# A second, transposed copy of x for 31 of the 48 token tiles of a hybrid encoder layer on eight cores

## The reference

```
def _rmsnorm(x, g):
    y = x * rsqrt(mean(x * x, axis=-1) + 1e-6) * g

hn = _rmsnorm(x, norm_g)
proj = einsum('bsd,de->bse', hn, w_in)
q, k, v, z_a, hc, gb, gc, z_b, g = split(proj)
...
u = gc * hc
conv = conv_w[0] * up[:, :-2] + conv_w[1] * up[:, 1:-1] + conv_w[2] * up[:, 2:]
c = (silu(z_b) * (gb * conv)) @ w_conv_out
```

## Time and profile before

| | |
|---|---|
| median of 3 runs | 1511.72 us (1510.96 to 1669.54) |
| the profiled execution | 1512.84 us, slowest core's span 1511.3 us |
| spans of the eight cores | 1508.7 to 1511.3 us |
| PE busy | 98% of the span |
| DVE, ACT, POOL busy | 62%, 46%, 10% |
| convolution steps | from about 27 us to about 270 us of the span |

### The profile page before, as it was taken

The page is one execution under the profiler, slowest core; times in us unless marked ns, Lnnn a source line. Parts: engine busy times, 40 slices in busy tenths (PEclk is TensorE's granted clock), DMA queues, the critical chain, the costliest instruction groups (busy, mean ns, idle before and its releaser), DMA issues.

```text
span 1511.3 us, 28483 instructions; the slowest of 8 cores (1508.7 to 1511.3 us)
## 1 busy us (share of the span) xinstructions
PE 1476.7 (98%) x11360; PEld 847.4 (56%) x11360; DVE 930.4 (62%) x1493; ACT 697.5 (46%) x1169; POOL 144.4 (10%) x286
## 2 busy tenths in 40 slices
PE   4999999999999999999999999999999999999997
PEld 2454445577666666675866665766444444444443
DVE  4677777335775848667569575686854444445445
ACT  4445454344575656645356557465322322232222
POOL 5212113000010000100000000001100000000001
PEclk9999999999999999999999999999999999999999
DMA  9964554413151431512425115154943233243233
GB/s 253 153 125 103 117 106 78 72 39 83 29 104 18 96 56 26 95 16 40 87 63 104 29 23 107 26 101 67 190 105 101 84 107 91 82 111 101 67 112 125
DMA packets 67764, 132.07 MB, mean 87 GB/s; under 512 B 8752, under 2 KB 34480, under 8 KB 67376
## 3 DMA queue, kind: packets, MB, share of 16 engines
q1 hardware_dynamic: 49296, 96.70, 23.8%
q0 software_dynamic: 18336, 33.56, 16.3%
HBM read 130.17 MB, written 33.62 MB: 108 GB/s over the span
## 4 chain that ended last, share of the span: by engine, by line
PE 90%; DMA 4%; DVE 3%; issue 1%; ACT 1%; POOL 1%; SPq 0%; DVEq 0%; POOLq 0%; ACTq 0%
PE ps L407 53%; PE ps L702 10%; PE ps L1092 7%; PE ps L1122 6%; PE ps L858 6%; PE ps L722 4%; PE ps L811 3%; DMA X<-w_in 2%; PE ps L452 1%; DMA gc_s<-X 1%; DMA X<-xw 1%; DVE X L908 1%; DVE X L833 0%; POOL stat L421 0%; SPq L163 0%
## 5 line engine op out<-in xcount | busy, mean ns | idle before, releaser
L407 PE MATMUL ps<-hnT,wbf 128*128 128x512 bf16 (+1 forms) x3008 | 666.2, 374 | 1.8 <-ACT X L397 0.8
L407 PEld LDWEIGHTS ps<-hnT,wbf 128*128 128x128 bf16 x3008 | 282.4, 98 | 312.1 <-issue 2.9
L397 ACT ACTIVATE X<-ps 128x512 bf16<-128x512 f32 (+2 forms) x320 | 219.4, 694 | 198.0 <-PE ps L407 157.6
L823 ACT ACTIVATE X<-ps 128x512 bf16<-128x512 f32 x384 | 204.3, 615 | 116.8 <-PE ps L811 116.8
L407 PE MATMUL ps<-hnT,X 128*128 128x512 bf16 (+1 forms) x1152 | 245.6, 367 | 0.1
L873 DVE TENSOR_TENSOR X<-ps,X 128x512 f32<-128x512 f32 x128 | 110.9, 867 | 157.8 <-PE ps L858 118.4
L407 PEld LDWEIGHTS ps<-hnT,X 128*128 128x128 bf16 x1152 | 107.9, 98 | 125.6 <-DMA X<-w_in 0.5
L1097 DVE SCALAR_TENSOR_TENSOR hnT<-hnT,ps 128x512 f32<-128x512 f32 x128 | 87.0, 685 | 146.5 <-PE ps L1092 145.0
L833 DVE TENSOR_TENSOR X<-X,et 128x512 bf16<-128x512 bf16 x384 | 146.0, 419 | 37.4 <-ACT X L823 36.3
L702 PE MATMUL ps<-wbf,hnT 128*128 128x128 bf16 x2720 | 164.6, 220 | 0.0
L702 PEld LDWEIGHTS ps<-wbf,hnT 128*128 128x128 bf16 x2720 | 159.2, 114 | 3.3
(11 more groups left out here) (60 smaller groups left out, 985.3 us busy)
## 6 DMA issues: line engine op xcount, KB each, us to landing
X<-xw SPq DMA_DIRECT2D x80, 512.0 KB, 6.1
wbf<-w_in POOLq DMA_DIRECT2D x95, 256.0 KB, 6.4
y<-X SPq DMA_DIRECT2D x31, 512.0 KB, 3.9
X<-w_in POOLq DMA_DIRECT2D x17, 256.0 KB, 19.3
ga_s<-X SPq DMA_DIRECT2D x32, 128.0 KB, 4.3
X<-ga_s SPq DMA_DIRECT2D x8, 512.0 KB, 8.7
X<-gc_s SPq DMA_DIRECT2D x8, 512.0 KB, 9.2
gc_s<-X SPq DMA_DIRECT2D x24, 128.0 KB, 6.0
```

What stands on the lines that cost most here:

```text
L397: return op("act", lambda e: e.activation(out=out, in_=in_, func=AF.Copy), reads=reads, writes=writes)
L407: fns.append(lambda e, kt=kt: e.matmul(bv.cols(c0, n), lhsT=wf(kt), rhs=hnT.cols(kt * WT + t0, n), start=(kt == 0), stop=(kt == 7)))
L823: op("act", lambda e, bv=bank(sb_ + hh), hh=hh: e.activation(out=prv.cols(hh * 512, 512), in_=bv.cols(0, 512), func=AF.Exp, scale=0.125), ...
```

## The change

The host now lays x down a second time, as `xt`: for each group of 512 tokens four pieces of 128 channels by 2 blocks by 512 tokens, 512 KB each. The first 17 tiles of the loading order go through the five stages as before, but from the tenth on their loads go round four buffers (`xk`) and not six. The other 31 tiles are handled in eight groups, seven of four tiles and one of three (`group_events`):

- the tiles are still loaded with tokens on partitions (three buffers, SP's queue) and squared and summed; POOL now writes the reciprocal roots of a group side by side into `rs`;
- `store` writes these four columns to DRAM (`rs_s`), where they lie as one row of 512 in token order, and `spread` loads that row into all 128 partitions (`rb_`, 256 KB); both are on SP's queue, and the second waits for the first to land;
- four pieces of `xt` are loaded through POOL's queue into three `xa` buffers and the one that held the gains, and DVE multiplies each in two halves of 512 columns by the gain (a column) and by the row of reciprocal roots, straight into `hnT` (L520 of the changed kernel).

Neither T nor E is left for these tiles. Groups are 2.57 steps apart, counted now in steps; the pieces' loads come due 2.4 steps ahead of their multiplication. From step 9 on events are also emitted in the middle of a step (`mid`), and the store of the step before goes ahead of the events at a step's end.

```
+            xk = i % 6 if i < 9 else (i + 2) % 4
...
-        order = [8, 9, 10, 11, 7] + list(range(12, 41)) + list(range(0, 7)) + list(range(41, 48))
+        order = [8, 9, 10, 11, 7] + list(range(12, 24))
...
-                p1ev.append((i + sk, -rank_, i, fn))
+                p1ev.append((8 + (i + sk - 21.5) / 1.3, -rank_, i, fn))
...
+        def group_events(k, G, nt):
+            t0, n, p = 5.6 + 2.57 * k, 128 * nt, k % 2
...
+                at = t0 + 0.64 * t
+                p1ev.append((at, 0, 100 + k, load))
+                p1ev.append((at + 1.9, 0, 100 + k, square))
+
+            def store():
+                dma("sp", "d_rs%d" % p, bass.AP(rs_d, 512 * k, [[nt, 128], [1, nt]]), rs4.cols(4 * p, nt),
+                    reads=[R_rs4[p]], writes=[R_rsd[k]])
+
+            def spread():
+                dma("sp", "d_rb%d" % p, rb.v.cols(0, n), bass.AP(rs_d, 512 * k, [[0, 128], [1, n]]),
+                    reads=[R_rsd[k]], writes=rb.r)
+            p1ev.append((t0 + 4.0, 0, 100 + k, store))
+            p1ev.append((t0 + 4.45, 0, 100 + k, spread))
+            for q in range(4):
+                def load(q=q):
+                    dma("pool", "d_xp%d" % q, xp_[q].v.base, bass.AP(xt_d, (4 * G + q) * 128 * 1024, [[1024, 128], [1, 1024]]),
+                        writes=xp_[q].r)
+
+                def norm(q=q):
+                    for j in range(2):
+                        op("dve", lambda e, j=j: e.scalar_tensor_tensor(
+                            out=hnT.cols((2 * q + j) * WT + 512 * G, n), in0=xp_[q].v.cols(512 * j, n),
+                            scalar=cf.cols(CF_G + 2 * q + j, 1), in1=rb.v.cols(0, n), op0=ALU.mult, op1=ALU.mult),
+                           reads=xp_[q].r + rb.r + [R_const], writes=hres(512 * G, 512 * G + n))
+                p1ev.append((t0 + 3.1 + 0.64 * q, 0, 100 + k, load))
+                p1ev.append((t0 + 5.5 + 0.64 * q, 0, 100 + k, norm))
+
+        for k, (G, nt) in enumerate(((6, 4), (7, 4), (8, 4), (9, 4), (10, 4), (1, 3), (0, 4), (11, 4))):
+            group_events(k, G, nt)
...
-                    conv_step(ct, c)
+                    conv_step(ct, c, mid=(lambda: p1_until(stepi + 0.5)) if stepi > 8 else None)
                     stepi += 1
-                    p1_until(21.5 + (stepi - 8) * 1.3)
-                    stores.pop(0)()
+                    if stepi > 8:
+                        stores.pop(0)()
+                    p1_until(stepi)
+                    if stepi <= 8:
+                        stores.pop(0)()
```

More of the change, by code:

```diff
@@ L207, in build_program @@
     k_d = [nc.dram_tensor("k_s%d" % g, [128, KOV[g] * 128], BF16) for g in range(3)]
+    rs_d = nc.dram_tensor("rs_s", [8, 512], F32)
     v2_d = nc.dram_tensor("v2_s", [128, 32 * VB_T], BF16)
@@ L223, in build_program @@
         stat_t = sb("stat", [128, 32], F32)
+        rs_t = sb("rs", [128, 8], F32)
         cbf_t = sb("cbfs", [128, 256], BF16)
@@ L276, in build_program @@
         R_patt = Res()
+        rs4 = View(rs_t[:])
+        R_rs4 = [Res(), Res()]
+        R_rsd = [Res() for _ in range(8)]
         R_gad = [[Res() for _ in range(8)] for _ in range(4)]
@@ L294, in build_program @@
         gb_ = xb(71040, 4096, F32)
+        rb_ = [xb(75136 + 2048 * i, 2048, F32) for i in range(2)]
+        xp_ = xa[3:6] + [gb_]
         xn_ = [xb(75136 + 2048 * i, 2048, BF16) for i in range(4)] + [Buf(View(et_t[:, 1536:2560]), [R_et[1]])]
@@ L411, in build_program, with rms_stat @@
         stat_ctr = {"i": 0}
-        def rms_stat(src, src_res, junk=junk_, eng="pool"):
+        def rms_stat(src, src_res, junk=junk_, eng="pool", out=None):
             k = stat_ctr["i"] % 8
@@ L422, in rms_stat @@
                                                  scalar2=EPS, op0=ALU.mult, op1=ALU.add), reads=[r], writes=[r])
-            op(eng, lambda e: e.tensor_tensor(out=stat.cols(c0 + 2, 1), in0=stat.cols(c0 + 1, 1),
-                                                 in1=cf.cols(CF_MH, 1), op=ALU.pow), reads=[r, R_mh], writes=[r])
-            return stat.cols(c0 + 2, 1), r
+            dst, dres = out if out is not None else (stat.cols(c0 + 2, 1), r)
+            op(eng, lambda e: e.tensor_tensor(out=dst, in0=stat.cols(c0 + 1, 1),
+                                                 in1=cf.cols(CF_MH, 1), op=ALU.pow), reads=[r, R_mh], writes=[dres])
+            return dst, dres
         R_gb = gb_.r
         def p1_stages(i, ti):
-            xt, xsem = xa[i % 6], "d_xa%d" % (i % 6)
+            xk = i % 6 if i < 9 else (i + 2) % 4
+            xt, xsem = xa[xk], "d_xa%d" % xk
             xn = xn_[i % 5]
@@ L471, in build_program, with load, square @@
             for (sk, rank_, fn) in stages:
-                p1ev.append((i + sk, -rank_, i, fn))
+                p1ev.append((8 + (i + sk - 21.5) / 1.3, -rank_, i, fn))
+        tring = {"i": 0}
+        def group_events(k, G, nt):
+            t0, n, p = 5.6 + 2.57 * k, 128 * nt, k % 2
+            rb = rb_[p]
+            for t in range(nt):
+                st = {}
+                def load(t=t, st=st):
+                    c = tring["i"] % 3
+                    tring["i"] += 1
+                    st["b"] = xa[c]
+                    dma("sp", "d_xa%d" % c, st["b"].v.base, bass.AP(xw, (512 * G + t) * D, [[nt * D, 128], [1, D]]),
+                        writes=st["b"].r)
+                def square(t=t, st=st):
+                    rms_stat(st["b"].v.base, st["b"].r, xn_[2], out=(rs4.cols(4 * p + t, 1), R_rs4[p]))
+                at = t0 + 0.64 * t
[21 more added lines that the diff above has]
+                p1ev.append((t0 + 5.5 + 0.64 * q, 0, 100 + k, norm))
@@ L1314 @@
             flags[:, 3] = -1.0
-        cfp = np.ascontiguousarray(np.concatenate([cw, flags, bg], axis=1).astype(np.float32))
-        in_maps.append({"xw": xwin, "w_in": w_in2, "w_ao": w_ao, "w_co": w_co, "w_o": w_o2, "gvec": gvec,
+        cfp = np.ascontiguousarray(np.concatenate([cw, flags, bg, gcol], axis=1).astype(np.float32))
+        xt = np.ascontiguousarray(xwin.reshape(XROWS // 512, 512, 4, 2, 128).transpose(0, 2, 4, 3, 1)).reshape(
+            XROWS // 512, 4, 128, 1024)
+        in_maps.append({"xw": xwin, "xt": xt, "w_in": w_in2, "w_ao": w_ao, "w_co": w_co, "w_o": w_o2, "gvec": gvec,
                         "fgvec": fgvec, "cfp": cfp, "cbf": cbf, "etab": _CACHE["etab"]})
```

10 lines of the change are left out of this document (6 added, 4 removed).

## The result

The changed kernel takes 1564.4 us (median of four runs, 1562.0 to 1566.9) where the kernel before took 1511.3 on the same chip: 1.0349 times as long, with a 95% interval of 1.0336 to 1.0362. It is slower by 53 us, and outside the forecast range of 1497 to 1524 us.

The account below looks back on a forecast made before the run. PE was taken as the bound, busy for 98% of the slowest core's span. 1512.8 - 13.8 + 6 + 2 = 1507 for the profiled execution, 1.1 above the median, gave 1506 us, range 1497 to 1524.

Parts of the forecast that it names:

- Transposes, -13.8: Phase 1, PE: 31 tiles lose their transposes at 0.445 us each, saving 13.8 us, all of which counts.
- Early chain, +6: Steps 1 to 7: ring of four delays loads, gc_s stores, then DVE and PE; +6 us, bounds -2 to +12.
- Price of all this: +2 us: Group phase: DVE's new waits at a group's multiplications cost PE +2 us, between 0 and Rival 2's price.
- 87% of what was seen: Group phase: DMA demand of 269 GB/s set against 309, the trace's fullest window.
- the store of four columns (2.6 ...): Each group, SP: this store lands in 2.6 us, within 11.1 us from last square to spread row.
- Both have more than a step of room: Group phase: waits on SP behind the store's landing, and POOL's roots behind xt loads, each have over a step of room.
- Rival 2: Steps 9 to 31: convolution store landings bound; slower beyond 7.6 us; 1519 to 1554; with Rival 3 0.25 below 2%, 0.05 above.
- the right signs: Behind step 9 PE waits for DVE's L522 or L532, with DVE itself waiting for gc_s at L550.
- its own formula: Rival 2's cost: (landing - 6.91) x 23 - 12 us; 13 us at 8.0, 48 at 9.5.
- a piece arrives alone every 4.4 us: Group phase: argument against Rival 2, pieces come singly and not four loads at once.
- Rival 3: Group phase: DVE at 96% load becomes the bound, 1525; chance counted with Rival 2, 0.25 below 2%, 0.05 above.
- Rival 4: Change does not do what it says and PE keeps waiting at other tiles; answered no, no chance given.

Follow-up runs that it names:

- e9: Changed kernel with xt pieces loaded for the first group only, gc_s stores and spread free of waits on SP, ring of six: 0.9936 of the kernel before.
- e1: Kernel before, with only the loads of tiles 9 to 16 going round four buffers instead of six: 1.0061 of the kernel before.
- e6: Changed kernel with the first 17 tiles' loads going round six buffers again: 1.0330 of the kernel before.
- e5: Changed kernel with each gc_s store recording only its own piece and the spread reading x from HBM, so neither waits for a store's landing: 1.0127 of the kernel before.
- e10: e5 with the spread reading 128 different rows of x instead of one row 128 times: 1.0145 of the kernel before.
- e4: Changed kernel with xt pieces loaded for the first group only, a minimum replacing the second product: 1.0120 of the kernel before.
- e11: Changed kernel, nothing left out: own record per gc_s store, ring of six, spread emitted later behind its store, pieces and multiplications a step later: 1.0167 of the kernel before.
- e7: Changed kernel with half of each xt piece loaded after the first group, in as many DMAs, a minimum replacing the second product: 1.0196 of the kernel before.
- e2: Changed kernel with each gc_s store recording only its own piece, so no store waits for the one before: 1.0423 of the kernel before.
- e3: Changed kernel with the spread reading 512 columns of x from HBM, waiting for nothing: 1.0223 of the kernel before.
- e8: Changed kernel with ring of six and only the last 15 tiles, in four groups, handled the new way: 1.0223 of the kernel before.
- e12: e8 with own record per gc_s store, groups 2.57 steps apart and the groups' events moved: 1.0354 of the kernel before.

## Why the prediction was wrong

**Transposes, -13.8: right in kind and in size.** e9 has the removal with little else, and its group phase takes 182.9 us for the 183.0 reckoned; at the end 10 us of the 13.8 are left. In the changed kernel the time went into waits.

**Early chain, +6: right, and then worth nothing.** The stores, the buffers and the transpose were the ones named, step 8 began at 94.69 where it was 90.44, 4.3 us later. e1 measured about 7 for it in the kernel before. Yet e6, without it, ended no sooner: the group phase behind has a bound of its own and takes in what is won ahead of it. The sum added two terms that don't add.

**"Price of all this: +2 us": the step that failed.** The group phase takes 244.2 us and not 183.0, so this term was 61 us. Three sentences under it were wrong.

- *"87% of what was seen".* The demand of 269 GB/s was held against 309, the best 5 us of the start, which carry another mix of transfers. e5 moves 216 to 228 GB/s here at a share of 0.94 to 0.98. As an estimate, at 222 the 4.8 MB of a group take 21.6 us and not 17.8: 3.8 us for each of eight groups, 30 us. e5 stands 19 above before and 29 above e9 (which has the ring of six too), and that agrees. The profile had a warning: 106 GB/s at a share of 0.54 is 196 at a full one, from 35 to 65 us the share was full at 166, and over its first 50 us the kernel before moved 232 at 0.99. By each of them a demand of 269 is too much, though none is the ceiling of the new mix. The Trainium skill's page "DMA: Bandwidth & Descriptors", section "Bandwidth", gives some 358 GB/s for a core of a streaming pair. With eight cores and this mix the runs show less: 216 to 235 over 50 us on the slowest cores of e5 and e10 at shares of 0.94 to 0.98, and 265 at most on any core (e10, core 7, 175 to 225 us, share 0.99). Its rule that another engine's queue adds no bandwidth (section "Rules for kernel authors") agrees with the runs: with the pieces on POOL's queue the stores on SP's land after 8.4 us for 5.9 before, and in e4, without the pieces, after 6.6.
- *"the store of four columns (2.6 ...)".* The shortest landing of any store was taken for one in a full stretch; it was 6.4 (median), 12.0 in the group of three tiles, and the spread 7.2 for the 6 reckoned. The chain from the last square to the row is then 16 us for 11.1, and DVE's wait at the first multiplication 41.1 us in seven, not 0 to 4 each.
- *"Both have more than a step of room".* A step of room was reckoned for each wait alone. But on SP they come one behind the other: in a group 2.57 landings of 8.4 and one of 6.4 make 28 us of waits, less what overlaps, for 17.8 us of work. Measured is 244.2 / 24 = 10.2 us a step, 26.2 a group. POOL's room was spent too: it stood 118.1 us at the loads of the pieces, waiting for DVE's multiplications to free them, with the next roots behind it.

So there are two causes of about one size. The waits on SP are worth 34 us (e5, and 28 in e11 with nothing left out), the pieces 35 (e4, 23 to 47; half of their bytes 23, e7), both with the ring 62 (e9). Inside the first the parts don't add: freeing the stores alone gave nothing (e2), the spread alone 19 us (e3). And the two are linked: landings get longer with the load (SP waited 155 us for them, and 106 in e4 in the same order), and a queue that waits pays each one in full.

**The clock was not in the sum.** On core 4, 14.7 of the 61 us are the same work at a lower granted clock, once PE had begun to stall. No term and no rival had it; the earlier trace rows, at 1.00 all through, could not show it. In e9, where PE hardly stands, the clock is 1.00 in every window read. What it cost beside the stalls is open, since core 0, at 0.84, was through with the phase earlier.

**Rival 2 named the right queue and the right signs, but half of the mechanism.** The signs came: PE waits for DVE's L578, DVE for `gc_s` at L606, and a landing of 8.4 us is past its point of decision (7.6; its own formula gives 7.7). The formula gives (8.4 - 6.91) x 23 - 12 = 22 us, 1528, and the run is 36 above that. But e2 takes away just what the formula rests on, the wait of a store for the store before it, and wins nothing; the gain of 34 us comes only when the spread is free of its 2 KB store as well (e5), and that pair is not in the rival. It got 0.05 above 2% on the argument that "a piece arrives alone every 4.4 us"; that spaces the bytes, but takes none away.

**Rival 3 fell.** DVE was busy for 62% from 100 to 250 us and not for over 90%, and idle because it waited; e9 ran it at 93% without harm. **Rival 4** was rightly put at no.

Open is why in e8 and e12 the DMA engines were busy for 0.89 to 0.95 of the time at 136 and 137 GB/s, what sets the 216 to 235 elsewhere, why the clock stays low on some cores only, and whether half of the groups at another place, clear of the next phase's weights, would win anything. None of the versions with the whole computation is faster than the kernel before.

## What to carry to other kernels

Ask of a change that trades compute for transfers what the DMA engines do in that very stretch, and measure the demand against long windows with a full share (here 166 and 232 GB/s, and 196 by dividing a row's GB/s by its share), not against the best few microseconds (309). These still scatter: e5 and e10 reached 216 to 235, and e12 only 136 beside weight loads. In an in-order queue add up the landings that are waited for, one behind the other, at the landing times of the loaded state, and hold the sum against the length of a round; room for each wait alone says nothing. And a gain ahead of a stretch that has a bound of its own is not a term of the sum.

## What the hardware showed that was not expected

A granted clock can stay low while PE never rests. These are windows of core 1, the slowest, in e7:

```profile
60.00:80.00 20.00, 14.94 (x94) 7.66 (x93) 12.96 (x24) 6.85 (x11) 1.48 (x4) 0.91 0.27 73
100.00:150.00 50.00, 50.00 (x192) 20.67 (x191) 29.36 (x55) 18.08 (x33) 15.07 (x27) 0.81 0.70 179
150.00:200.00 50.00, 50.00 (x192) 20.73 (x191) 38.29 (x69) 16.84 (x30) 14.48 (x29) 0.81 0.74 176
```

PE is busy for all of 100 us at 0.81, and does 192 matmuls in 50 us where e9 does 228 to 230 at 1.00. Core 6 of the same execution had 0.97 in both windows, with PE idle now and then. So busy PE at 100% is not PE at full speed, and on this core the slow clock set the pace of the step.

The trace does not say why. What the engine did before the clock fell was to stand 5.1 us for DVE's L454. But all eight cores stood there, for 4.0 to 5.3 us, and from 80 to 150 us the clock was low on cores 0 and 1 alone. Core 5, which stood longest, reads:

```profile
80.00:100.00 20.00, 20.00 (x126) 10.07 (x125) 15.49 (x27) 8.51 (x14) 2.19 (x4) 1.00 0.43 118
```

In e1 and e12 too a lower mean clock comes on two neighbouring cores together (2 and 3, and 6 and 7, in the profiled run of e12), and goes with some 20 us. That is as much as some differences between experiments, so read the clock of every core before comparing two kernels by their slowest.

The 2 KB store of 128 rows of 16 bytes took 6.4 us to land in the median, where 256 KB took 7.2. In e4, with less traffic, it took 4.9, and in e5 11.8: in a loaded stretch a landing depends more on the load than on the size.
